# Encoder block on one core: convolution tables loaded behind the last projection tile, router products turned, last backward decay in its own buffer

## What is computed

```python
hn = rmsnorm(x, g)
p = hn @ w_in                       # 2560 columns: lru_x | lru_gate | v | x1 | x2, 512 each
xc = dwconv4(lru_x)
h  = rg_lru(xc, forward) + rg_lru(xc, backward)
     # r, i = sigmoid gates;  a = exp(-8 r softplus(-lambda))
     # s[t] = a[t] s[t-1] + sqrt(1 - a[t]^2) i[t] xc[t]
yA = h * gelu(lru_gate)
v, x1, x2 = dwconv3(p[:, 1024:])
z  = x1 * (fftconv(v, h1) + skip1 * v)
yB = x2 * (fftconv(z, h2) + skip2 * z)
x  = x + concat(rmsnorm(yA), rmsnorm(yB)) @ w_out
f  = rmsnorm(x, g_ffn)
lg = f @ [router_group_w | router_expert_w] + bias      # 4 + 32 = 36 logits for each token
x  = x + top2_of_8_experts_in_top1_of_4_groups(f, lg)
out = rmsnorm(x, g_final)
```

## Time and profile before

| what | value |
|---|---|
| three runs | 2252.47, 2252.68, 2256.26 us; median 2252.68 |
| the profiled execution | 2250.65 us, with a span of 2248.9 us from its first to its last instruction |
| mean granted TensorE clock of it | 0.957 of full speed |
| busy in the span | PE 2041.7 us (91%), DVE 1215.8 (54%), ACT 1113.8 (50%), POOL 360.5 (16%) |
| transfers | 476.90 MB, mean 212 GB/s |

### The profile page before, as it was taken

One profiled execution on the slowest core, in us unless ns is written; L12 is line 12 of the kernel. 1 busy time (PEld: TensorE's weight loads), 2 busy tenths in 40 slices (PEclk: granted clock), 3 DMA queues, 4 the chain that ended last, 5 costly groups with the idle time before them and its releaser, 6 DMA issues. The chain is left out here.

```text
span 2248.9 us, 30873 instructions
## 1 busy us (share of the span) xinstructions
PE 2041.7 (91%) x9293; PEld 1452.3 (65%) x9294; DVE 1215.8 (54%) x1123; ACT 1113.8 (50%) x1315; POOL 360.5 (16%) x323
## 2 busy tenths in 40 slices
PE   3999999999998877979999499999999999999990
PEld 2437777777665222327878378888787788888870
DVE  6653322236666634744444664566868666565644
ACT  6871222226666231432333164566868666565633
POOL 0780000000000220320000012122121122111120
PEclk9999999999999988979999689999999999999995
DMA  5790231221234998866442467788999988886848
GB/s 215 249 322 27 85 85 52 85 75 40 61 75 125 341 342 320 284 205 218 169 150 91 153 196 254 219 293 285 375 309 374 336 281 262 291 281 207 290 142 317
DMA packets 240654, 476.90 MB, mean 212 GB/s; under 512 B 25121, under 2 KB 87717, under 8 KB 235431
## 3 DMA queue, kind: packets, MB, share of 16 engines
q1 hardware_dynamic: 201800, 383.62, 47.5%
q0 software_dynamic: 15424, 58.78, 10.8%
q10 hardware_dynamic: 23360, 33.56, 4.6%
HBM read 355.24 MB, written 114.29 MB: 209 GB/s over the span
## 5 line engine op out<-in xcount | busy, mean ns | idle before, releaser
L1820 PE MATMUL p<-wh_hi,x_hi 128*128 128x512 f32 x768 | 308.0, 401 | 1.8 <-DVE x_lo L1934 0.6
L1820 PE MATMUL p<-wh_hi,x_lo 128*128 128x512 f32 x768 | 303.7, 395 | 0.0
L1820 PE MATMUL p<-wh_lo,x_hi 128*128 128x512 f32 x768 | 303.3, 395 | 0.0
L1946 DVE TENSOR_TENSOR wh_lo<-w_raw,wh_hi 128x2048 fp32r<-128x2048 f32 x128 | 284.8, 2287 | 27.4 <-ACT wh_hi L1907 27.4
L537 PE MATMUL ps<-h_hi,wp_hi 128*128 128x512 f32 x640 | 256.9, 401 | 4.3 <-DVE wp_lo L730 4.3
L537 PE MATMUL ps<-h_lo,wp_hi 128*128 128x512 f32 x640 | 253.6, 396 | 0.0
L537 PE MATMUL ps<-h_hi,wp_lo 128*128 128x512 f32 x640 | 253.6, 396 | 0.0
L1907 ACT ACTIVATE wh_hi<-w_raw 128x2048 fp32r<-128x2048 f32 x128 | 234.7, 1922 | 0.4 <-DMA w_raw<-in_exp_w_dram 0.4
L1820 PEld LDWEIGHTS p<-wh_hi,x_hi 128*128 128x128 f32 x768 | 144.4, 188 | 36.1 <-issue 1.7
L1820 PEld LDWEIGHTS p<-wh_hi,x_lo 128*128 128x128 f32 x768 | 144.2, 188 | 35.8
L1820 PEld LDWEIGHTS p<-wh_lo,x_hi 128*128 128x128 f32 x768 | 144.5, 188 | 33.4
(11 more groups left out here) (314 smaller groups left out, 3488.1 us busy)
## 6 DMA issues: line engine op xcount, KB each, us to landing
w_raw<-in_exp_w_dram SPq DMA_DIRECT2D x512, 256.0 KB, 6.0
w_raw<-in_exp_w_dram SPq DMA_DIRECT2D x128, 512.0 KB, 11.2
dec<-in_decay_dram SPq DMA_DIRECT2D x32, 512.0 KB, 5.6
scratch_KA<-work SPq DMA_DIRECT2D x32, 512.0 KB, 4.4
scratch_SI<-arena SPq DMA_DIRECT2D x32, 512.0 KB, 3.5
kin<-scratch_KA SPq DMA_DIRECT2D x21, 512.0 KB, 6.3
arena<-scratch_SA SPq DMA_DIRECT2D x21, 512.0 KB, 5.3
wp_raw<-in_w_in_dram SPq DMA_DIRECT2D x18, 512.0 KB, 3.7
```

Of the source, the lines that this page charges most:

```text
L1820: mm = pe.matmul(acc[:, :], x[:, k, :], w, start=(k == 0 and i == 0), stop=(k == n - 1 and i == 2))
L1946: dve.tensor_tensor(lo, raw[:, j:j + 2, :], hi.bitcast(F32), ALU.subtract).then_inc(lowered, 1)
```

## The change

1. **Loads.** The rest of the tables `fwd` and `inv` and the rows of blocks 1 and 2 (6.0 MB) were issued on SP once the last projection tile was done. They are now issued after the first, second and third chunk of that tile.
2. **Decay.** For c of 1 to 3 the backward `decay` writes the buffer xc in place of Q and waits for `weighed` (the last read of xc) in place of the forward scan.
3. **Last scan.** It stands ahead of the products of block 0; `add_last` moves from block 3 to 2, `gate_last` from 6 to 4.
4. **w_out.** Its loads move from blocks 9, 11, 13, 15 to blocks 16, 18, 20, 22; `high` is in blocks 20 to 27, `low` in 21 to 28.
5. **Router.** The logits are taken for two tiles at once: the router columns, padded with zeros to 64, are stationary, and the hidden tiles (256 columns) move. Even k go to rows 0 to 63 of the result, odd k to rows 64 to 127. ACT copies that (`copy_logits`), PE sums the two halves and turns the result back with a matrix `both` (`fold`, two products), and DVE adds the bias for two tiles.

```diff
+        decayed = lambda c, d: xc if c and d else Q
...
+                     last_chunk=lambda n: after(place["g", CT - 1], n))
...
             def decay(c, d):
                 act.wait_ge(evac, after(gate_place[c] + (1 if c else 2 * d)))
-                if d:
-                    act.wait_ge(scanned, 2 * c + 1)
+                if d and c:
+                    act.wait_ge(weighed, c)
+                elif d:
+                    act.wait_ge(scanned, 1)
                 elif c:
                     act.wait_ge(y_out, 16 * c)
                 else:
                     act.wait_ge(tst_out, 16 * 2 * CT)
-                act.activation(Q, T[d], ACT.Exp, scale=col_of(Q_EXP[d], c, d)).then_inc(exp_ready, 1)
+                act.activation(decayed(c, d), T[d], ACT.Exp, scale=col_of(Q_EXP[d], c, d)).then_inc(exp_ready, 1)
...
                 lru_input(c, 0)
-                lru_scan(0)
+                lru_scan(c, 0)
                 if c + 1 < CT:
                     low(TILES.index(("x", c + 1)) + 1)
                 lru_input(c, 1)
+                lru_scan(c, 1)
                 if c + 1 == CT:
                     break
-                lru_scan(1)
                 if c == 0:
                     add_directions(c)
+                else:
+                    dve.wait_ge(scanned, 2 * c + 2)
                 lru_conv(c + 1)
                 low(TILES.index(("g", c)) + 1)
                 if c:
                     add_directions(c)
                 gate_result(c)
-            marks.update(scan_last=lambda: lru_scan(1), add_last=lambda: add_directions(CT - 1), gate_last=lambda: gate_result(CT - 1))
+            marks.update(add_last=lambda: add_directions(CT - 1), gate_last=lambda: gate_result(CT - 1))
...
+            sp.wait_ge(marks["mm_done"], marks["last_chunk"](0))
+            sp.dma_start(fwd[:, 2:4, :], dram["fwd_b"][:, 2:4, :]).then_inc(fwd_in[1], 16)
+            sp.dma_start(fwd[:, 4:, :], dram["fwd_b"][:, 4:, :]).then_inc(fwd_in[2], 16)
+            sp.wait_ge(marks["mm_done"], marks["last_chunk"](1))
+            for n in (1, 2):
+                sp.dma_start(kin[n], pair_rows("KA", n)).then_inc(kin_in[n], 16)
+            sp.dma_start(inv[:, 0:EARLY], dram["inv_b"][:, 0:EARLY]).then_inc(inv_in[0], 16)
+            sp.wait_ge(marks["mm_done"], marks["last_chunk"](2))
+            for n in (1, 2):
+                sp.dma_start(zin[n], pair_rows("SA", n)).then_inc(zin_in[n], 16)
+            sp.dma_start(inv[:, EARLY:], dram["inv_b"][:, EARLY:]).then_inc(inv_in[1], 16)
...
-                    if n < PAIRS and n > 8 and n % 2:
-                        load_wo((n - 9) // 2)
+                    if n >= PAIRS and n % 2 == 0 and n < PAIRS + 8:
+                        load_wo((n - PAIRS) // 2)
...
             sp.wait_ge(marks["mm_done"], marks["projected"])
-            load_k(1)
-            sp.dma_start(fwd[:, 2:4, :], dram["fwd_b"][:, 2:4, :]).then_inc(fwd_in[1], 16)
-            load_z(1)
-            sp.dma_start(inv[:, 0:EARLY], dram["inv_b"][:, 0:EARLY]).then_inc(inv_in[0], 16)
-            load_k(2)
-            sp.dma_start(fwd[:, 4:, :], dram["fwd_b"][:, 4:, :]).then_inc(fwd_in[2], 16)
-            load_z(2)
-            sp.dma_start(inv[:, EARLY:], dram["inv_b"][:, EARLY:]).then_inc(inv_in[1], 16)
             blocks(0)
...
-                    if n > PAIRS and n % 2:
-                        high((n - PAIRS) // 2)
+                    if PAIRS + 4 <= n < PAIRS + 4 + KC:
+                        high(n - PAIRS - 4)
...
-                if n == 0:
-                    marks["scan_last"]()
-                if n == 3:
+                if n == 2:
                     marks["add_last"]()
-                if n == 6:
+                if n == 4:
                     marks["gate_last"]()
...
-                if n % 2 == 0 and n > PAIRS:
-                    low((n - PAIRS) // 2 - 1)
-            low(KC - 1)
+                if PAIRS + 5 <= n < PAIRS + 5 + KC:
+                    low(n - PAIRS - 5)
...
+            def logits(n, tiles=slice(0, 2)):
+                pe.wait_ge(hT_ready, 4 * n + 2 * tiles.stop)
+                at_least(pe, lg_copied, n)
+                at_least(pe, lg_ready, n)
+                pe.wait_ge(ms, min(2 * n + 4, NT))
                 for k in range(KC):
-                    last = pe.matmul(pl, hT[:, k, :], rw[:, k, :], start=(k == 0), stop=(k == KC - 1))
+                    rows = slice(k % 2 * R, k % 2 * R + R)
+                    last = pe.matmul(lgT[rows, tiles.start * P:tiles.stop * P], rw[:, k, :], hT[:, k, tiles, :].rearrange("p t n -> p (t n)"),
+                                     start=(k < 2), stop=(k >= KC - 2))
                 last.then_inc(lg_mm, 1)
+
+            def fold(n):
+                pe.wait_ge(lg_copied, n + 1)
+                at_least(pe, lg_ready, n)
+                pe.wait_ge(ms, min(2 * n + 5, NT))
+                for i in range(2):
+                    last = pe.matmul(pl[:, i, :], lgS[:, i * P:(i + 1) * P], both[:, :], start=True, stop=True)
+                last.then_inc(folded, 1)
...
+                if t >= 3:
+                    if t % 2:
+                        logits((t - 3) // 2)
+                    else:
+                        fold((t - 4) // 2)
...
+                if t == NT - 1:
+                    fold(NT // 2 - 2)
...
-            logits(NT - 2)
+            logits(NT // 2 - 1, slice(0, 1))
             transposes(NT - 1)
-            logits(NT - 1)
+            logits(NT // 2 - 1, slice(1, 2))
+            fold(NT // 2 - 1)
...
+            def copy_logits(n):
+                act.wait_ge(lg_mm, n + 1 + n // (NT // 2 - 1))
+                at_least(act, folded, n)
+                act.activation(lgS[:, :], lgT, ACT.Copy).then_inc(lg_copied, 1)
...
+            def add_bias(n):
+                dve.wait_ge(folded, n + 1)
+                dve.tensor_tensor(LG[:, 2 * n:2 * n + 2, :], pl, rb[:, :].unsqueeze(1).broadcast_to([P, 2, NL]), ALU.add).then_inc(lg_ready, 1)
```

More of the change, by code:

```diff
@@ L409, in project_and_lru @@
         steps = sem("p_steps")
-        pt_swapped, xc_exchanged, weighed, exchanged = (sem(n, 0) for n in ("pt_swapped", "xc_exchanged", "weighed", "exchanged"))
+        weighed = sem("weighed", 0)
+        pt_swapped, xc_exchanged, exchanged = marks["pool_dma"]
         yield sem
@@ L455, in project_and_lru @@
         marks.update(weighed=weighed, xraw=xraw, WG=WG, fs=fs, mm_done=mm_done, evac=evac, tr_evac=tr_evac, xc_ready=xc_ready, sa_out=sa_out,
-                     gates_done=after(gate_place[CT - 1] + 3), projected=after(place["g", CT - 1]))
+                     gates_done=after(gate_place[CT - 1] + 3), projected=after(place["g", CT - 1]),
+                     last_chunk=lambda n: after(place["g", CT - 1], n))
         block = yield
@@ L765, in lru_input, with lru_scan @@
                 dve.wait_ge(exp_ready, 2 * c + d + 1)
-                step(dve.scalar_tensor_tensor(out=I[d], in0=Q, scalar=1.0, in1=I[d], op0=ALU.add, op1=ALU.mult))
+                step(dve.scalar_tensor_tensor(out=I[d], in0=decayed(c, d), scalar=1.0, in1=I[d], op0=ALU.add, op1=ALU.mult))
                 dve.wait_ge(sqrt_ready, 2 * c + d + 1)
                 step(dve.tensor_tensor(I[d], T[d], I[d], ALU.mult))
-            def lru_scan(d):
+            def lru_scan(c, d):
                 o = slice(None, None, -1) if d else slice(None)
-                dve.tensor_tensor_scan(T[d][:, o], Q[:, o], I[d][:, o], 0.0, ALU.mult, ALU.add).then_inc(scanned, 1)
+                dve.tensor_tensor_scan(T[d][:, o], decayed(c, d)[:, o], I[d][:, o], 0.0, ALU.mult, ALU.add).then_inc(scanned, 1)
             def add_directions(c):
@@ L1252, in output_projection @@
         pz, small = bank("pz5"), bank("small5")
-        pl, psq = small[:, 0:NL], small[:, P:P + 2]
+        lgT, pl, psq = small[:, 0:2 * P], small[:, 2 * P:2 * P + 2 * NL].rearrange("p (t n) -> p t n", n=NL), small[:, 3 * P:3 * P + 2]
+        assert nc.sbuf_base <= marks["w_at"] and marks["w_at"] + 72 * 1024 <= nc.sbuf_usable_end
         N_W = 5
@@ L1380, in _ @@
                 half(t, 0, pA, projA)
-                if t == 2:
+                if t == 3:
                     pe.wait_ge(par_in, 16 * N_W)
-                if t >= 2:
-                    logits(t - 2)
+                    pe.wait_ge(both_ready, 1)
+                if t >= 3:
[3 more added lines that the diff above has]
+                        fold((t - 4) // 2)
                 if t + 1 < NT:
@@ L1431, in _ @@
                     second_half(t + 1)
+                if t >= 3 and t % 2:
+                    copy_logits((t - 3) // 2)
                 if t:
@@ L1494, in _ @@
                     split_a(t + 1)
-                if t >= 2:
-                    add_bias(t - 2)
+                if t >= 4 and t % 2 == 0:
+                    add_bias((t - 4) // 2)
                 if t + 1 < NT:
@@ L1505, in _ @@
                                              op0=ALU.mult, op1=ALU.add).then_inc(x2_ready, 1)
+                if t == NT - 1:
```

(6 more changed lines are left out.)

25 lines of the change are left out of this document (12 added, 13 removed).

## The result

The changed kernel takes 2227.05 us in the median (2224.28 to 2228.8, four runs), the one before 2252.57 in the same comparison: a ratio of 0.9884, with a 95% interval of 0.9867 to 0.9902. The forecast was 2225, faster. The profiled execution has a span of 2226.9 us, where that of before had 2248.9.

What follows compares the result with a forecast made beforehand. PE, busy for 91% of the span, was taken to lose conv time at its start and first pass's end. Terms 16.0 + 2.6 + 1.6 - 1.0 + 0.65 + 7.5 + 0 = 27.4 off 2250.65 gave 2223.2, median 2225, range 2218 to 2238.

Steps and rivals of the forecast that it cites:

- The start: Conv's first pass up to block 3's signal product: early loads and moved scan together gain 16.0 us (12 to 16.5).
- 8 us, with the queue nearly empty: Block 3's rows at the conv's start: loaded about 726, needed at 734; if late, a loss up to 4 us.
- Rival D: Conv start: gap closes only in part, block 3's rows behind large loads; keeps 5.1 us, total 2230; chance 0.10.
- The end of the first pass: Conv blocks 11 to 15: without w_out's loads a gain of 2.6 us (1.4 to 4.6).
- The turnaround: After the first pass: the last store lands sooner without a w_out load ahead, gain 1.6 us (0.5 to 2.5).
- The second pass: Blocks 16 to 23, where w_out's 4 MB now fall: a loss of 1.0 us (0 to 4.6).
- Rival B: Second pass: w_out's transfers stall it as they did the first, 4.6 us lost, total 2229; chance 0.17.
- Rival E: Second pass starves and PE falls to the 1.2 GHz level; slower, total 2269; chance 0.03.
- The last products: End of the second pass: last products no longer stand behind a `low`, gain 0.65 us.
- The router: Output projection loop: a pair's logits cost 2.4 us instead of 3.48, seven pairs gain 7.5 us.
- Rival C: Router: column halves do not run side by side for 256 columns, loses 3.6 us, total 2236; chance 0.09.
- The end of the stage: End of the output projection: two half logits, copy and fold replace two logits, 0 us (-1 to 0.5).

Runs made afterwards that it cites:

- late_exchange: Changed kernel with the last exchange behind POOL's subtraction of block 1, and add_last and gate_last two blocks later; 2232.01 us.
- loads_only: Kernel before with the early loads alone; decay, scan, w_out loads and router as before; 2251.09 us, ratio 0.9983 to before.
- scan_only: Kernel before with the decay in its own buffer, the last scan ahead of block 0, add_last and gate_last moved; 2257.04 us, ratio 1.0004.
- old_router: Changed kernel with the router of before, all edits of output_projection undone; 2232.79 us.
- wo_first: Changed kernel with w_out's four loads back in blocks 9, 11, 13 and 15 of the first pass; 2232.01 us.
- wo_double: Changed kernel with four more 1 MB loads in blocks 17, 19, 21 and 23, twice the transfers of w_out; 2229.56 us.
- k_first: Changed kernel with SP loading a block's filter rows ahead of its signal rows; 2224.81 us.
- late_k: Changed kernel with both the edits of late_exchange and k_first; 2228.38 us.
- one_half: Changed kernel with all eight router products of a pair on columns 0 to 63, the fold summing over 64 rows; 2239.91 us.
- the second comparison: The changed kernel unedited, run once more beside variants and the kernel before; 2224.17 us, ratio 0.9867.

## Why the prediction was right, and where not

**The start** is right in mechanism and size: 15.04 for 16.0, with every step of it: decay, scan, products (1.77 behind z0 for 1.82), first inverse 6.96 behind z0 for 7.0, block 2 at 8.88 for 9.0. The missing 1.0 is block 3's filter rows. "8 us, with the queue nearly empty" was the step that failed: the queue holds the exchange that the change itself moved ahead to this place. The rows were issued 2.41 us behind z0 and took 9.3 us to land in the changed kernel, and 5.0 in late_exchange, where the exchange comes later (transfers issued there, the changed kernel first):

```profile
xraw<-scratch_KA SPq DMA_DIRECT2D x1, 512.0 KB, 9.3
xraw<-scratch_KA SPq DMA_DIRECT2D x1, 512.0 KB, 5.0
```

Rival D forecast late rows of block 3, but behind large loads and not beside the exchange, and it is no rival but a spread: the wait is 0.85 to 1.08 us in five profiles, and 3.95 in one, where block 3 follows block 2 by 11.3 us instead of 5.5, which is more than D's 5.1. That the two parts are worth so much only together was not priced in the prediction; loads_only and scan_only show it.

**The end of the first pass** is right (2.55 for 2.6). **The turnaround** was taken too small, 3.36 for 1.6. The store's part is 2.5 (840.07 - 834.78 = 5.29 before, 823.94 - 821.15 = 2.79 after), at the good end of the term's range. The other 0.86 is the last inverse, which took 2.85 us before and 1.99 after, and it is luck: the granted clock was 0.68 there before (830.80 to 833.70) and 1.00 after (818.00 to 820.10), and in the other kernels with the moved loads the same inverse takes from 1.99 to 3.45 us (old_router).

**The second pass** lost 0.26, not 1.0, in the first profile. Over the kernels it takes 82.0 to 84.3 us with the moved loads (eight profiles) and 82.0 to 83.4 with the loads in the first pass (five). But much of that spread is block 16 alone, which follows a wait of 6.3 to 6.5 us and takes 4.8 to 6.5. From block 17's signal product to block 31's, all five kernels with the loads in the first pass take 76.97 us, wo_first among them, which differs from the changed kernel in the place of these loads alone. Six of the eight with the moved loads take 77.26 to 78.07, with small waits such as this one of old_router (PE's timeline):

```profile
931.99 1.94 PE L998 MATMUL ps<-kin,fwd_b 128*64 128x512 f32 x8 [0.43 <-DMA kin<-scratch_KA]
```

So a loss is there, 0.3 to 1.1 us, and the forecast of 1.0 was right in kind and near in size; wo_double has 82.66. The two others, k_first and late_k, load a block's filter rows ahead of its signal rows and take 76.97 again, so that this order seems to take the loss away; two profiles are few. Rival B, with 4.6, is out at this load, and wo_double says how near it is. The Trainium skill's 358 GB/s for transfers between HBM and SBUF ("DMA: Bandwidth & Descriptors", section "Where 436 GB/s comes from") did not bind here. The 372 and 406 GB/s of the windows above count stores too, but from 715 to 727 the changed kernel has only loads in its queues (columns as in rows 1):

```profile
715.00:727.00 12.00, 12.00 (x52) 9.21 (x52) 11.90 (x5) 10.39 (x10) 0.00 (x0) 1.00 1.05 405
```

Rival E is out too: the clock stayed at 1.00 with PE waiting 0.7 us in each block.

**The last products** came out as said (the last inverse starts 6.16 us behind block 31's signal product, 6.81 before), but the 0.65 was not gained: the next stage then waits for its table `ia`, 12.45 us instead of 11.93 (PE's timelines, before and after):

```profile
997.75 1.98 PE L1334 MATMUL pz<-stage,ia 128*64 128x512 f32 x4 [11.93 <-DMA ia<-in_inv_a_dram]
983.32 1.97 PE L1346 MATMUL pz<-stage,ia 128*64 128x512 f32 x4 [12.45 <-DMA ia<-in_inv_a_dram]
```

The step that failed was to count a gain in front of a wait for a transfer.

**The router** is right: a pair costs (15.90 - 13.86) + (14.26 - 13.86) = 2.44 us, forecast 2.4, and loop and end of the stage together gain 7.09 for 7.5. The change of tiling mode that the prediction set against this edit shows as no more than some 0.1 us: a tile with the logits grows by 2.04 us and the products take 1.95. (A steady conv block, by which the prediction bounded it, changes mode twice and not three times: the filter and signal products are of one form, the inverse of another.) Rival C would have cost 11 us, as one_half shows. The end of the stage is 0.63 worse for a forecast of 0, inside its -1 to 0.5.

**The total** of the first profile is 22.0 us, 5.4 less than the sum. 4.83 of that stands ahead of the first edited instruction in the conv, and 4.24 of it is there when the projection's second tile starts (200.60 and 204.84 us), long before any edited instruction of the recurrence, whose first decay begins at 530. Over the 14 profiles z0 lies from 723.5 to 728.3, the first profile of before at one end and that of the changed kernel at the other, and old and new code are found on both sides; so I take it for a difference between executions, not for an effect of the change. By medians the gain is 25.5 (2252.57 - 2227.05), and 29.5 in the second comparison (2253.68 - 2224.17). The forecast lies in between. What remains open is the middle stage: 47.8 to 51.3 us over the kernels, with waits of 0.5 to 3.7 us for staged rows that come and go, in unedited code.

No variant beats the changed kernel by what can be measured.

## What to carry to other kernels

Before a stage can start early, all of its bounds have to go: list the chain of engines and the queue of loads separately, with the time at which each would release the same instruction, and expect little from an edit that removes one of them alone (here 5.2 and -0.9 us of 15.0). A transfer that is moved ahead to unblock one engine falls among the transfers of another; ask which rows it then delays. Gains add up only as far as the next wait for a transfer.

## What the hardware showed beyond that

With POOL's exchange in the queues the transfers go slowly though the engines are busy. A window of scan_only, against the 406 GB/s at 1.04 above:

```profile
737.00:746.00 9.00, 0.04 (x2) 0.04 (x2) 0.00 (x0) 0.00 (x0) 0.70 (x1) 0.50 1.00 250
```

The DMA share is 1.00, and 250 GB/s move, while the large table of 1792 KB took 18.5 us to land (10.3 with the exchange held back). The other kernels show the same with the exchange in flight: 242 GB/s at 0.97 in the changed kernel (730.5 to 739), 249 at 1.01 in late_exchange (738 to 750), 223 at 1.02 in k_first (729 to 741).

And behind the longer waits of PE the next products took up to twice their time (3.68 us for 1.89 behind 12.35 us in scan_only, 2.46 and then 3.11 behind 3.95 in old_router, 3.06 and 2.51 behind 4.06 in late_exchange), so that waits of 3.95 and 4.06 us lengthened a block by 5.8 and 5.9 in all. The granted clock fell there: it was 0.50, the lower of its two levels, over the slow product of scan_only, and 0.70 on the mean over the 5.6 us behind the waits of the other two (738.4 to 744 and 752.4 to 758).

```profile
745.90:750.00 4.10, 4.04 (x10) 1.20 (x12) 0.00 (x0) 0.00 (x0) 0.00 (x0) 0.50 1.02 428
```

Behind the waits of 0.66 to 1.08 us the products took 1.94. Behind waits of 3.2 us both are found: 1.94 in the kernel before, 3.28 in wo_first.
